# Five buffers for the first weight blocks, wider small products, and squares added later, in a fused transformer kernel

## The reference

```python
for i in range(2):                                   # first block
    sh1, sc1, g1, sh2, sc2, g2 = split(silu(c) @ ada_w[i] + ada_b[i], 6)
    h = rmsnorm(x, norm1_g[i]) * (1 + sc1) + sh1
    if i == 0:   # mixer: h @ w_in -> latents; q, k, v from rmsnormed latents; per-head
                 # rmsnorm of q and k; rotary; softmax attention over 512 keys; a short
                 # convolution beside it; the concatenation @ w_o
        out = even_mixer(h, h_ctx, w_in, w_uq, w_ukv, ..., w_o)
    else:        # Fourier transform over tokens and features, then @ w_fourier
        out = fourier_mixer(h, w_fourier)
    x = x + g1 * out
    x = x + g2 * swiglu(rmsnorm(x, norm2_g[i]) * (1 + sc2) + sh2, ffn_w1[i], ffn_w3[i], ffn_w2[i])
# second block: windowed attention beside a gated linear recurrence, then a
# mixture of 32 experts (top 4 of each token), then a final rmsnorm
```

## Time and profile before

| | |
|---|---|
| median of 3 runs | 1797.28 us (1795.56 to 1797.48) |
| profiled execution | 1793.97 us, its span 1792.2 us |
| TensorE busy | 1652.7 us (92%) |
| VectorE busy | 751.9 us (42%) |
| ScalarE busy | 432.0 us (24%) |
| GpSimd busy | 118.5 us (7%) |
| moved by DMA | 586.35 MB, mean 327 GB/s |

### The profile page before, as it was taken

The page is one execution under the profiler, slowest core; times in us unless marked ns, Lnnn a source line. Parts: engine busy times, 40 slices in busy tenths (PEclk is TensorE's granted clock), DMA queues, the critical chain, the costliest instruction groups (busy, mean ns, idle before and its releaser), DMA issues.

```text
span 1792.2 us, 22044 instructions
## 1 busy us (share of the span) xinstructions
PE 1652.7 (92%) x8358; PEld 993.4 (55%) x8358; DVE 751.9 (42%) x1186; ACT 432.0 (24%) x642; POOL 118.5 (7%) x151
## 2 busy tenths in 40 slices
PE   5899899999989999999999999999978898899775
PEld 2863588888778888877433433344423342344222
DVE  5566578877478776654211221222201120112012
ACT  3434644453344544342000000000000000000001
POOL 1752010000500000020000000000000000000000
PEclk8998999999999999998999999999989998899888
DMA  8623559886459787508999999999999999999995
GB/s 341 242 97 104 201 180 341 315 296 210 177 200 340 291 324 278 203 24 333 396 421 421 420 421 420 420 420 421 421 420 420 421 421 421 420 420 421 420 421 203
DMA packets 103503, 586.35 MB, mean 327 GB/s; under 512 B 12369, under 2 KB 13649, under 8 KB 50801
## 3 DMA queue, kind: packets, MB, share of 16 engines
q1 hardware_dynamic: 103408, 585.09, 82.6%
HBM read 584.00 MB, written 1.05 MB: 326 GB/s over the span
## 4 chain that ended last, share of the span: by engine, by line
PE 74%; SPq 10%; DMA 8%; DVE 4%; issue 2%; ACT 1%; POOL 1%; DVEq 0%; ACTq 0%
PE psum L1257 21%; PE psum L1273 10%; SPq L434 8%; PE psum L924 4%; PE psum L925 4%; PE psum L926 4%; PE psum L1232 3%; PE psum L1042 3%; PE psum L945 2%; PE psum L947 2%; PE psum L946 2%; PE psum L1286 2%; DMA araw<-ada_dram 2%; PE psum L1138 2%; DMA mraw<-dn_dram 2%
## 5 line engine op out<-in xcount | busy, mean ns | idle before, releaser
L1257 PE MATMUL psum<-mraw,xsat 128*64 128x512 f32 (+2 forms) x1544 | 423.6, 638 | 37.0 <-DMA mraw<-gu_dram 25.2
L1257 PEld LDWEIGHTS psum<-mraw,xsat 128*64 128x64 f32 (+2 forms) x1544 | 140.4, 144 | 260.6 <-issue 259.0
L1273 PE MATMUL psum<-mraw,xsat 128*64 128x512 f32 (+2 forms) x680 | 176.1, 625 | 14.2 <-DMA mraw<-dn_dram 6.3
L1257 PE MATMUL psum<-mlast,xsat 128*64 128x512 f32 (+2 forms) x408 | 149.2, 657 | 16.9 <-DMA mraw<-gu_dram 16.9
L924 PE MATMUL psum<-wh,ah 128*128 128x512 f32 x352 | 139.6, 397 | 2.6 <-DVE al L1928 1.8
L926 PE MATMUL psum<-wh,al 128*128 128x512 f32 x352 | 137.3, 390 | 0.0
L925 PE MATMUL psum<-wl,ah 128*128 128x512 f32 x352 | 137.3, 390 | 0.0
L1814 POOL TENSOR_TENSOR wl<-raw,wh 128x256 fp32r<-128x256 f32 x132 | 107.4, 848 | 388.6 <-DVE work L1955 219.8
L2462 DVE TENSOR_TENSOR oacc<-psum,oacc 128x512 f32<-128x512 f32 x60 | 38.6, 686 | 214.0 <-PE psum L1286 214.0
L1976 DVE TENSOR_TENSOR wl<-raw,wh 128x1024 fp32r<-128x1024 f32 x88 | 103.6, 1219 | 32.8 <-ACT wh L1538 32.8
L1273 PEld LDWEIGHTS psum<-mraw,xsat 128*64 128x64 f32 (+2 forms) x680 | 55.8, 138 | 105.2 <-issue 104.2
(11 more groups left out here) (380 smaller groups left out, 2523.5 us busy)
## 6 DMA issues: line engine op xcount, KB each, us to landing
mraw<-gu_dram SPq DMA_DIRECT2D x193, 1024.0 KB, 21.5
mraw<-dn_dram SPq DMA_DIRECT2D x85, 1024.0 KB, 24.4
araw<-ada_dram SPq DMA_DIRECT2D x128, 512.0 KB, 5.1
mlast<-gu_dram SPq DMA_DIRECT2D x51, 1024.0 KB, 19.9
raw<-ffa_dram SPq DMA_DIRECT2D x44, 1024.0 KB, 5.1
mlast<-dn_dram SPq DMA_DIRECT2D x34, 1024.0 KB, 24.5
raw<-ffb_dram SPq DMA_DIRECT2D x44, 512.0 KB, 5.3
raw<-blk_dram SPq DMA_DIRECT2D x34, 512.0 KB, 4.8
```

The source lines that it names most:

```text
L1257: last = mm(ps[4 + n][a * w:(a + 1) * w, :], xs[:, k * P + a * w:k * P + (a + 1) * w], slot_columns(slot, i * 2 * D + n * 512), start=Fals ...
L1273: last = mm(ps[n][a * w:(a + 1) * w, :], at[:, k * P + a * w:k * P + (a + 1) * w], slot_columns(slot, i * D + n * 512), start=(k == 0), st ...
```

## The change

- `w_in`'s blocks get five slots in `raw` (`NFIRST_RAW`), block b waiting for the split of block b-5. SyncE's queue is reordered: blocks 3 and 4 go out once the third ada pair is read, `uk` and the constants `cone` once the fourth is, blocks 7 to 10 ahead of ada chunk 18, and `uq` last, once block 14 is split, under a semaphore of its own for which `q_product` waits.
- `ada_columns` makes products of 64 equal columns, where it made one of one column, spread over bank 2; `mod_ready` reads every 64th.
- `spread` takes all 128 rows of the constant (zero below row 8) and of `rt`.
- `keep_clock` is called with 5 products ahead of block 0 and with 4, in bank 0, ahead of the first scores, behind a wait for the copied values.
- `add_square` moves behind the residual update and comes later: squares 1, 2, 3 and 4, 5 after updates 4, 5, 6, 7; in the second layer squares 1, 2 and 3, 4 and 5, 6.
- The division in attention stays on ScalarE, as it was.

```diff
-NRAW = 3
+NRAW, NFIRST_RAW = 3, 5
-RAW = [(5120 if b >= B_O + NRAW else 0) + (b % NRAW) * D for b in range(B_2)]
+RAW_SLOT = [b % NFIRST_RAW if b < B_O else (b - B_O) % NRAW for b in range(B_2)]
+RAW_LOADED = [16 * (RAW_SLOT[:b + 1].count(RAW_SLOT[b]) + (RAW_SLOT[b] >= NRAW)) for b in range(B_2)]
+RAW = [(5120 if b >= B_O + NRAW else 0) + RAW_SLOT[b] * D for b in range(B_2)]
...
-        MLA_IN, DFT_IN, LRU_IN, EXP_IN = 48, 64, 64 + 256, 64 + 256 + 32
+        MLA_IN, DFT_IN, LRU_IN, EXP_IN = 32, 48, 48 + 256, 48 + 256 + 32
...
+        s_raw, s_uq = s_raw + s_afirst[1:3], s_afirst[0]
...
             def blk(b):
-                if b >= NRAW:
-                    sp.wait_ge(s_hi, b - NRAW + 1)
-                    sp.wait_ge(s_lo, b - NRAW + 1)
-                sp.dma_start(raw[:, RAW[b]:RAW[b] + D], blk_d[b]).then_inc(s_raw[b % NRAW], 16)
+                if b >= NFIRST_RAW:
+                    before = b - (NFIRST_RAW if b < B_O else NRAW)
+                    sp.wait_ge(s_hi, before + 1)
+                    sp.wait_ge(s_lo, before + 1)
+                sp.dma_start(raw[:, RAW[b]:RAW[b] + D], blk_d[b]).then_inc(s_raw[RAW_SLOT[b]], 16)
...
             for b in range(NRAW):
                 blk(b)
 
+            sp.wait_ge(s_adp, 3)
+            for b in range(NRAW, NFIRST_RAW):
+                blk(b)
             ada(ADA_FIRST)
             ada(ADA_FIRST + 1)
-            for b in range(NRAW, 6):
+            for b in range(NFIRST_RAW, 7):
                 blk(b)
-            sp.wait_ge(s_adp, 8)
-            sp.dma_start(uq, uq_d).then_inc(s_par, 16)
+            sp.wait_ge(s_adp, 4)
             sp.dma_start(uk, uk_d).then_inc(s_par, 16)
             sp.dma_start(cone[:, :], cone_d).then_inc(s_par, 16)
-            blk(6)
-            blk(7)
+            for b in range(7, 11):
+                blk(b)
             for n in range(2, 8):
+                blk(9 + n)
                 ada(ADA_FIRST + n)
-                blk(6 + n)
-            for b in range(14, B_O + 3):
+            blk(17)
+            sp.wait_ge(s_lo, 15)
+            sp.dma_start(uq, uq_d).then_inc(s_uq, 16)
+            for b in range(B_O, B_O + NRAW):
                 blk(b)
             ada(24)
...
                 for i in range(8):
-                    last = mm(ps[2][:, i:i + 1], acc[:, i * P:(i + 1) * P], ones[:, 0:1], start=True, stop=True)
+                    last = mm(ps[2][:, 64 * i:64 * i + 64], acc[:, i * P:(i + 1) * P], ones[:, 0:64], start=True, stop=True)
                 last.then_inc(s_acol, 1)
...
-            def keep_clock(n):
+            def keep_clock(n, bank=7):
                 for _ in range(n):
-                    mm(ps[7][:, 0:T], ones, con[:, 0:T], start=True, stop=True)
+                    mm(ps[bank][:, 0:T], ones, con[:, 0:T], start=True, stop=True)
...
+            keep_clock(5)
...
             def q_product(j):
+                pe.wait_ge(s_uq, 32)
...
-                mm(ps[PAIR_BANK[h % PAIRS]][0:QD, :], C("bcast8", 768, 8)[:, h * QD:(h + 1) * QD], rt[0:8, :],
+                mm(ps[PAIR_BANK[h % PAIRS]][0:QD, :], C("bcast8", 768)[:, h * QD:(h + 1) * QD], rt[:, :],
                    start=True, stop=True).then_inc(s_qkbc, 1)
...
+            pe.wait_ge(s_vc, 4)
+            keep_clock(4, 0)
             pe.wait_ge(s_qrope, 5)
             pe.wait_ge(s_qkn, HEADS)
...
             def block_hi(b):
-                act.wait_ge(s_raw[b % NRAW], 16 * (b // NRAW + 1))
+                act.wait_ge(s_raw[RAW_SLOT[b]], RAW_LOADED[b])
                 wait(act, s_blk, SPLIT_BEFORE[b])
                 A(wh[:, SPLIT[b] * D:(SPLIT[b] + 1) * D], raw[:, RAW[b]:RAW[b] + D], ACT.Copy).then_inc(s_hi, 1)
...
             def mod_ready(g):
                 dve.wait_ge(s_acol, g + 1)
-                TTn(mod[:, 8 * g:8 * g + 8], ps[2][:, 0:8], bias(g), ALU.add).then_inc(s_mod, 1)
+                TTn(mod[:, 8 * g:8 * g + 8], ps[2][:, :].rearrange("p (i a) -> p i a", a=64)[:, :, 0], bias(g), ALU.add).then_inc(s_mod, 1)
...
             for j in range(DJ):
-                if 2 <= j < 7:
-                    add_square(1, j - 1)
                 residual(B_O + j, j, 2)
+                for k in {4: (1,), 5: (2,), 6: (3, 4), 7: (5,)}.get(j, ()):
+                    add_square(1, k)
...
             for j in range(DJ):
-                if j >= 2:
-                    add_square(3, j - 1)
                 residual(B_F + j, j, 8)
+                for k in {4: (1,), 5: (2, 3), 6: (4, 5), 7: (6,)}.get(j, ()):
+                    add_square(3, k)
                 if j == 4:
                     wide_lo(1, 0, 0)
             wide_lo(1, 1, 1)
```

More of the change, by code:

```diff
@@ L52 @@
 SPLIT_BEFORE = [max([k + 1 for k in range(b) if SPLIT[k] == SPLIT[b]], default=0) for b in range(B_2)]
-RAW = [(5120 if b >= B_O + NRAW else 0) + (b % NRAW) * D for b in range(B_2)]
+RAW_SLOT = [b % NFIRST_RAW if b < B_O else (b - B_O) % NRAW for b in range(B_2)]
+RAW_LOADED = [16 * (RAW_SLOT[:b + 1].count(RAW_SLOT[b]) + (RAW_SLOT[b] >= NRAW)) for b in range(B_2)]
+RAW = [(5120 if b >= B_O + NRAW else 0) + RAW_SLOT[b] * D for b in range(B_2)]
 MIX_SLOT = (0, 1, 2, 5, 3, 6, 4, 7, 1, 2, 5)
-MIX_BASE = [16 * len(range(i, B_2, NRAW)) for i in range(NRAW)] + [16 * (1 + NF), 16 * (1 + NF), 0, 16 * (1 + NF), 16 * (1 + NF)]
+MIX_BASE = [16 * RAW_SLOT.count(i) for i in range(NRAW)] + [16 * (1 + NF), 16 * (1 + NF), 0, 16 * (1 + NF), 16 * (1 + NF)]
 MIX_LOADED = [MIX_BASE[s] + 16 * MIX_SLOT[:k + 1].count(s) for k, s in enumerate(MIX_SLOT)]
@@ L353, in build @@
         s_th, s_lruo = sem("lru_tanh"), sem("lru_out")
-        s_mix = s_raw + [s_fraw[0], s_fbraw[0], sem("mixer_blocks_loaded"), s_fraw[1], s_fbraw[1]]
+        s_mix = s_raw[0:NRAW] + [s_fraw[0], s_fbraw[0], sem("mixer_blocks_loaded"), s_fraw[1], s_fbraw[1]]
         s_xc = sem("xr_xg_copied")
```

## The result

The changed kernel takes 1776.74 us (median of 4 runs, 1776.03 to 1777.91); the kernel before, run beside it, took 1796.42 (4 runs, 1790.0 to 1797.48). The ratio is 0.9905, 95% interval 0.9878 to 0.9933. Forecast were 1779.3 and a range of 1774 to 1787. The profiled executions have spans of 1792.2 and 1776.1: 16.1 us of the forecast 18.0.

What follows compares the result with a forecast made beforehand. TensorE led the chain before 838 us; then the experts' weights stream at a fixed rate, so early savings count one to one. Terms 7.7 + 1.3 + 3.3 + 0.9 + 2.4 + 2.4 = 18.0 us gave 1779.3, range 1774 to 1787.

Steps and rivals of the forecast that it cites:

- Step 1: Block loads: the gap before block 11 goes and the key latents' sums run at full clock, 7.7 us.
- Step 2: Fill ahead of block 0 raises the clock earlier, 1.1 us; with block 7's GpSimd wait of 0.25 gone, 1.3 us.
- Steps 3 and 4: Key factors over 128 rows keep clock up, 3.3 us; fill ahead of first scores brings full clock, net 0.9 us.
- the first rival: Clock falls before the scores all the same, following only how busy TensorE is: time 1786.3 us, chance 0.14.
- Step 5: Modulation columns made 64 wide: taken as 0 us; 0.9 us each time if added in full.
- Step 6: Output blocks: squares added two updates later remove TensorE's 2.78 us wait, gaining 2.4 us in each layer.
- Late next is the block product: Output blocks: once the wait for squares goes, the block product limits, with one addition of some 0.4 us left.
- the second (GpSimd): GpSimd becomes the pace of the blocks, 0.5 us on each of the last eight: time 1783.4 us, chance 0.10.
- The fifth: SyncE's new order turns six ada loads into a series that VectorE waits on: slower, 1802.9 us, chance 0.03.
- The third: Attention is held by its ada loads and gives back 4.2 us: time 1783.5 us, chance 0.04.

Runs made afterwards that it cites:

- the buffers alone: Changed kernel with all edits undone except the five slots and SyncE's new queue order: 1784.84 us, ratio 0.9945 to the kernel before.
- the two best versions: Changed kernel with the modulation columns' fifth group and two adaLN updates earlier: 1770.61 us; the same without the fill ahead of the scores: 1771.74 us.
- the two other kernels with the old order: Changed kernel with squares ahead of the updates again, 1778.56 us; changed kernel keeping only the five slots and SyncE's new order, 1784.84 us.
- the experiment: Changed kernel with the key factors made from 8 rows again: 1779.65 us, ratio 0.9925 to the kernel before.
- the second trace of the changed kernel: Changed kernel run once more without any edit, beside other experiments: 1773.96 us, ratio 0.9896 to the kernel before.
- both kernels of 48.62 and 50.38: Changed kernel with the fifth column group and two adaLN updates earlier, with the fill ahead of the scores (1770.61 us) and without it (1771.74 us).

## Why the prediction was right, and where its steps were not

The forecast of 1779.3 was 2.6 us above the median. Part of that closeness is luck, since it was reckoned from a median of three runs and the last stage moves by more than 2.6; the gain that the traces assign is 16.1, not 18.0. The direction, the place and the way (an early stage starts the stream earlier) held: the ranking came 16 us sooner. Point by point:

- **Step 1 (7.7) held.** 7.98 measured between block 7 and block 17's end, of it 7.51 at block 10, where the gap lay, and the buffers with the new queue order alone give the same 43.14. No ada load stops VectorE there, and the query matrix was no wait: issued at 87.50, it is read behind 107, and TensorE waits for nothing from there to the first scores.
- **Step 2 (1.3) held between the two traces, and with it a good deal of chance.** 1.37 measured. In both traces block 0 begins 21.95 us behind the first sums and VectorE's last remainder ends at 26.19, so they compare well: block 0 takes 4.80 for 5.70 (0.9, forecast 1.1), and block 6 takes 2.88 for 3.29, so the wait at block 7 is gone (0.4, forecast 0.25). The clock was up when block 0 began (1.00 in 42.1 to 47.0), sooner than the step's sentence has it, by which it "should rise near 42.5", 1.7 us into block 0. What the step has not is that the fill may fail to keep the clock (three traces of ten), and that the clock ahead of it, in the row sums, moves VectorE's remainders by up to 1.3 us. For the same reason the 1.12 of the buffers alone isn't all theirs: 0.55 of it is that its last remainder came at 25.64.
- **Steps 3 and 4 (3.3 + 0.9) were right in sum and misplaced between them.** 4.10 measured from the first key product to the first maximum. The wide rows give 4.66, since they bring the scores to full clock too; the fill, which I credited with the scores, costs 0.56. Of the 4.66, 1.3 is there with the buffers alone, as the clock happened to fall later. That the rows of the products matter and not busy time alone is shown; the first rival's rule is not what these traces follow. Whether the fill pays in attention isn't settled: attention was 0.6 to 1.8 us shorter with it wherever neither kernel had half clock there and nothing else differed, and the two best versions, with and without it, are at 1770.61 and 1771.74, with intervals that overlap.
- **Step 5 (0) held.** Neither a cost nor a gain.
- **Step 6 (2.4 in each layer) held in the second and not in the first.** 2.67 and 0.97. The step that failed is "Late next is the block product": in layer 1 late next was VectorE with its adaLN updates, whose loads it waited for 4.3 us. With two updates and their loads earlier, the same edit gives 2.65. The 0.97 is also low because the kernel before lacked the half clock behind the wait that the two other kernels with the old order and these loads have; against them it is 2.1. The rows that I took for it showed only the wait removed, and I listed none for the loads that run in the same stretch.
- **The rivals.** The first (clock falls all the same) and the second (GpSimd) did not come: GpSimd's pieces grew to 898 ns and released no wait of TensorE in the blocks. The fifth did not either. The third did not come either: landings of adaLN loads have 43% of attention's chain, yet it was 1.0 shorter after the change and gave nothing back. The rest is in stretches without an edit, which vary by as much between traces of other kernels: the first stage was 1.3 longer and the stretch ahead of layer 2's output blocks 0.5 longer.

By the stretches, forecast against measured: 7.7 to 7.98, 1.3 to 1.37, 4.2 to 4.07, 4.8 to 3.64. The sum is 17.1 against 18.0, plus 0.98 in attention, less 1.32, 0.54 and 0.08 elsewhere: 16.1.

## What to carry to other kernels

When a wait is taken away, look in the same stretch for the load whose lateness it covered, and price that before counting the whole wait: the squares were worth 1.0 to 2.1 us with the loads late and 2.65 with them early, and moving two updates with their loads was worth 3.0 more. A product at the half clock costs time only where its operands come faster than it runs; compare the pitch of the rows at both levels before paying for a fill, and look at the last ones, where operands pile up: here the middle of the block gained nothing and its end 0.9 us. Where a late stage spreads by several microseconds from run to run, compare by the distance between two events on either side of the edit, and one trace can settle what five timed runs do not. But take the nearest events: the distance from the first sums to block 7 hid the fill's 0.9 behind operands that had come earlier, and the one from the last remainder to block 1 showed it.

## What was not expected of the hardware

- The granted clock fell behind stretches in which TensorE had no idle time but worked mostly on 8 rows (busy 5.50 of 5.50 us before the change, 3.63 of them in the factors; 5.40 of 5.40 in the experiment, all in them), and not where the same products had 128 rows (6.00 of 6.00): lower level 1.2 GHz against 2.4.
- The same five products of fill did not keep the clock in every trace: in the second trace of the changed kernel block 0 ran at 0.50 behind it, in the first at 1.00. In seven of ten traces it kept it.
- Attention took 48.6 to 50.5 us with the same instructions, at a clock of 1.00 in both kernels of 48.62 and 50.38. The share of adaLN landings in its chain (27% and 46% in these two) does not go along with the length over the other traces.
- The last stage, the same in every kernel, took 1084.7 to 1091.4 us. TensorE's busy time in it went along, at the same clock and the same bytes:

```profile
693.20:1777.90 1084.70, 993.08 (x4681) 459.10 (x4680) 267.03 (x556) 114.57 (x239) 10.95 (x15) 0.96 0.93 383
```
```profile
681.80:1773.20 1091.40, 999.96 (x4681) 465.10 (x4680) 267.09 (x556) 114.62 (x238) 10.95 (x15) 0.96 0.93 380
```
